# Feature-major stages of a two-block transformer kernel: the wide and the low product change places in every odd step of a tile

## The chip, the cores and the metric

The kernel runs on one core of one Trainium2 chip. The metric is the time of one execution in microseconds on the device. The kernel before took 3048.95 us, the median of three runs (3046.32 to 3049.08).

## The reference, cut to what matters

256 tokens of width 2048 go through two blocks in float32. The first block has a mixer of three kinds of attention, a gated feed-forward with a short convolution (`(gelu(conv(x @ w_gate)) * (x @ w_up)) @ w_down`, inner width 5632) and a gated extra projection. The second has stick-breaking attention and a state-space scan, and then a retrieval of experts (PEER): a query projection `q = (xt @ w_query)` with 2048 columns, scores against keys, a top-16, and the chosen rows of two tables of 16384 x 2048.

Two dense products matter here:

```
hg = x @ w_gate ; x @ w_up      # (256 x 2048) @ (2048 x 5632), twice
q  = (xt @ w_query)             # (256 x 2048) @ (2048 x 2048)
```

## The kernel before, in words

**Precision.** Every float32 operand is split into a high part (rounded to the format that TensorE multiplies) and a low part (the rest). A product is the sum of three: high weights with high activations, high weights with low activations, and low weights with high activations. The fourth, low with low, is left out.

**The stream of weights.** All weights come as units of 128 x 1024 floats (512 KB), in one fixed order over the whole kernel (`UNITS`). SyncE starts one DMA per unit into a slot of `raw` (line 546); ScalarE copies it to `whi` (the high part, line 652), VectorE subtracts to get `wlo` (the low part, line 1294), and TensorE waits in `weights(u)` for the low part, at the head of each unit. A unit's slot is free for the next DMA when TensorE has done its last matmul with it (`s_u`).

**The feature-major stages.** The function `fm_tiles` runs over tiles of 128 output features. A tile takes two units, each with eight of the 16 steps k over the 2048 input features. The result of a tile lies in one bank of PSUM, 128 features by two groups of 256 tokens. `fm_unit` is the function that writes the matmuls of one unit. In each step k it issues two, each with a weight load of its own:

- the wide one: high weights against the high and the low activations side by side, 512 columns, into the whole bank;
- the low one: low weights against the high activations, 256 columns, into the first half of the bank.

VectorE adds the two halves afterwards. Two stages use `fm_unit`: GU, the gate and up projection of the first block, with 88 tiles (line 2451), and WQ, the query projection of the second, with 16 tiles (line 2654). In GU the activations come from the tile `aa`, where the high and the low part lie apart; in WQ from `parts`, where they lie side by side. In both the weights are `whi` and `wlo`.

In steps 0 to 14 of a tile the wide matmul is issued first and the low one second. In step 15 the order is turned, because the last matmul of a tile has to be the one that writes the whole bank. So a tile ends with low 14, low 15, wide 15, and the next starts with wide 0.

The other stages have their own functions and aren't touched: `plain_unit` (all matmuls of 256 columns), `row_unit` (all of 512 columns), and `dn_unit` in the stage D of the second block, which has the same two kinds of product as `fm_unit`, of 384 and 192 columns, in the same order.

TensorE works its instructions off in the order written. Besides the unit it has small jobs of attention, transposes and the like, which `tasks.tick()` puts between units; in GU there are nearly none of them, in WQ there are some after every second tile or so.

Of the kernel before, what the change touches and what calls it, by code (L numbers as in the profile page):

```python
# [231 lines left out]
def build(nc, x, pT, colsd, w1fm, w1v, wo1, wgu, wdn, plg, plp, w2fm, w2v, wo2, wq, sk, dn, dnr, up, g5, out):  # L232
    ctx = ExitStack()
    with ctx:
# [191 lines left out]
        def parts(m, k):  # L426

            return PARTS[k] if m == 4 else AA[:, :, k, :]
# [1716 lines left out]
        def _(e):  # L2145
            tasks = Tasks()

            def mm(o, l, r, start=True, stop=True):
                return e.matmul(o, l, r, start=start, stop=stop)  # L2149
# [9 lines left out]
            def weights(u):  # L2159
                e.wait_ge(s_lo[SLOT[u]], TURN[u])  # L2160
                return WHI[SLOT[u]], WLO[SLOT[u]]
# [66 lines left out]
            def fm_unit(bank, free, m=None):  # L2228


                def unit(u, i, kh):
                    if kh == 0 and free(i) is not None:
                        e.wait_ge(*free(i))
                    w = weights(u)
                    b = B[bank(i)]
                    for kk in range(8):
                        k = kh * 8 + kk
                        hi, lo = [a[:, kk * 128:(kk + 1) * 128] for a in w]
                        if m is not None and i == 0:
                            e.wait_ge(n_al, 16 * m + k + 1)  # L2240
                        p = parts(m, k)
                        if k < 15:
                            mm(b, hi, p, k == 0, False)
                        last = mm(b[:, 0:256], lo, p[:, 0, :], False, False)
                        if k == 15:
                            last = mm(b, hi, p, False, True)
                    last.then_inc(s_u, 1)
                return unit

# [582 lines left out]
```

## Time and profile before

| | |
|---|---|
| median of three runs | 3048.95 us |
| span of the profiled execution | 3047.8 us |
| TensorE matmul busy | 3019.0 us (99%) |
| TensorE weight load busy | 2693.8 us (88%) |
| VectorE busy | 2318.9 us (76%) |
| ScalarE busy | 1676.8 us (55%) |
| mean granted TensorE clock | 0.999 |
| stage GU | from 468.7 to 966.4 us |
| stage WQ | from 1714.5 to 1815.2 us |

How to read it: the span is the time from the first to the last instruction of the one execution that the profiler recorded; for that execution no other time is given, and the runs behind the median are other executions. The weight load is a row of its own, since it runs beside the matmuls. A matmul's recorded duration includes its way through the array, so that consecutive ones overlap: what a matmul costs in a stream is the distance from its start to the start of the next.

### The profile page before, as it was taken

How to read it: one execution, taken by the hardware profiler on the slowest of the kernel's cores; microseconds unless marked ns; L12 is line 12 of the kernel's file. 1: busy time of each engine (PE TensorE's matmuls, PEld its weight loads, DVE VectorE, ACT ScalarE, POOL GpSimd, SP SyncE). 2: the span in 40 equal slices, each digit the busy share in tenths (PEclk: the TensorE clock that was granted, in tenths of full speed). 3: DMA queues.
4: the chain of work that ended last, by engine and by line, in shares of the span. 5: the costliest groups of instructions: out<-in, count | busy, mean ns of one | idle time of the engine just before them, and what ended most of it. 6: DMA issues, size and time to landing. Idle time of an engine off the chain costs nothing.

```text
span 3047.8 us, 44217 instructions
## 1 busy us (share of the span) xinstructions
PE 3019.0 (99%) x17678; PEld 2693.8 (88%) x17678; DVE 2318.9 (76%) x3482; ACT 1676.8 (55%) x2495; POOL 482.3 (16%) x316
## 2 busy tenths in 40 slices
PE   8999999999999999999999999999999999999999
PEld 7999988888888888889898889999999988888887
DVE  5477667777776454567767699999898898999987
ACT  5454655444444344554465545699965555555544
POOL 1000000000000000000000000033222333766642
PEclk9999999999999999999999999999999999999999
DMA  6543445555555555555344656788889999999996
GB/s 220 186 160 124 143 165 178 187 185 187 186 186 190 197 189 187 190 185 178 125 145 159 215 174 226 263 289 292 275 313 353 361 353 358 406 387 384 392 388 257
DMA packets 199213, 726.82 MB, mean 238 GB/s; under 512 B 22240, under 2 KB 22368, under 8 KB 198496
## 3 DMA queue, kind: packets, MB, share of 16 engines
q1 hardware_dynamic: 161280, 585.44, 54.0%
q0 software_dynamic: 37360, 136.79, 12.2%
q8 instruction: 141, 2.31, 0.3%
q10 hardware_dynamic: 368, 1.75, 0.2%
q14 instruction: 64, 0.52, 0.0%
HBM read 719.24 MB, written 4.19 MB: 237 GB/s over the span
## 4 chain that ended last, share of the span: by engine, by line
PE 91%; DVE 5%; ACT 2%; DMA 2%; issue 0%; SPq 0%; DVEq 0%; ACTq 0%
PE b L2149 90%; DVE wlo L1294 2%; DMA raw<-in_dn 1%; PE b L2157 1%; DVE ar L1283 1%; ACT ar L648 1%; ACT whi L652 1%; ACT oh L648 1%; DVE ar L1291 0%; DVE ar L1875 0%; DVE ar L1870 0%; DMA raw<-in_up 0%; DVE ar L1883 0%; DMA hsb<-in_x 0%; DVE ar L1867 0%
## 5 line engine op out<-in xcount | busy, mean ns | idle before, releaser
L1294 DVE TENSOR_TENSOR wlo<-raw,whi 128x1024 fp32r<-128x1024 f32 x1030 | 1251.4, 1222 | 489.1 <-ACT whi L652 485.8
L2149 PE MATMUL b<-aa,whi 128*128 128x256 f32 (+2 forms) x5824 | 1524.4, 340 | 4.3 <-DVE wlo L1294 4.3
L652 ACT ACTIVATE whi<-raw 128x1024 fp32r<-128x1024 f32 x1030 | 1075.8, 1055 | 666.1 <-DMA raw<-in_up 188.8
L2149 PE MATMUL b<-aa,wlo 128*128 128x256 f32 (+1 forms) x4640 | 1211.6, 269 | 0.0
L2149 PEld LDWEIGHTS b<-aa,whi 128*128 128x128 f32 x5824 | 1008.8, 190 | 75.2 <-issue 13.6
L2149 PEld LDWEIGHTS b<-aa,wlo 128*128 128x128 f32 x4640 | 882.0, 190 | 8.7
L2149 PE MATMUL b<-whi,asb 128*128 128x512 f32 x1092 | 366.2, 389 | 1.1 <-DVE ex L1283 1.1
L2149 PE MATMUL b<-whi,aa 128*128 128x512 f32 x1024 | 323.4, 393 | 2.1 <-DVE aa L1294 1.1
L638 POOL DMA_INDIRECT aaf<-in_up,ex x128 | 273.2, 2134 | 158.4 <-DVE aaf L1291 155.0
L2149 PE MATMUL b<-wlo,asb 128*128 128x512 f32 x728 | 283.2, 389 | 0.0
L627 POOL DMA_INDIRECT hsb<-in_dnr,ex x128 | 186.9, 1460 | 463.1 <-DVE small L2057 454.2
L2149 PEld LDWEIGHTS b<-whi,asb 128*128 128x128 f32 x1092 | 204.9, 188 | 44.0 <-DVE ex L1283 1.5
L2149 PEld LDWEIGHTS b<-whi,aa 128*128 128x128 f32 x1024 | 192.2, 188 | 43.1 <-issue 1.7
L648 ACT ACTIVATE ar<-ar 128x512 f32<-128x512 f32 (+5 forms) x212 | 112.3, 539 | 194.1 <-DVE ar L1291 117.2
L603 POOL MEMSET ar<- 128x384 f32 x1 | 0.4, 419 | 1309.5 <-ACT ar L649 1309.5
L2149 PE MATMUL b<-wlo,aa 128*128 128x512 f32 x512 | 199.3, 389 | 0.0
L1291 DVE SCALAR_TENSOR_TENSOR aaf<-aaf,ex 128x1024 f32<-128x1024 f32 x128 | 163.7, 1279 | 0.4 <-DMA aaf<-in_up,ex 0.3
L652 ACT ACTIVATE ar<-b 128x512 f32<-128x512 f32 (+2 forms) x99 | 53.0, 540 | 198.3 <-PE b L2149 163.0
L2149 PEld LDWEIGHTS b<-wlo,asb 128*128 128x128 f32 x728 | 136.7, 188 | 28.3
L2057 DVE CUSTOM_DVE_ANT_0 hsb<-hsb 128x1024 f32<-128x1024 f32 x128 | 155.8, 1218 | 0.1
L2149 PE MATMUL b<-whi,hth 128*128 128x512 f32 x352 | 137.1, 390 | 0.0
L2149 PE MATMUL b<-whi,htl 128*128 128x512 f32 x352 | 137.0, 389 | 0.0
(194 smaller groups left out, 2977.4 us busy)
## 6 DMA issues: line engine op xcount, KB each, us to landing
raw<-in_dn SPq DMA_DIRECT2D x256, 512.0 KB
raw<-in_up SPq DMA_DIRECT2D x182, 512.0 KB
raw<-in_wgu SPq DMA_DIRECT2D x176, 512.0 KB
raw<-in_wdn SPq DMA_DIRECT2D x88, 512.0 KB
raw<-in_w1fm SPq DMA_DIRECT2D x74, 512.0 KB
raw<-in_w2fm SPq DMA_DIRECT2D x74, 512.0 KB
raw<-in_wo SPq DMA_DIRECT2D x64, 512.0 KB
hsb<-in_up SPq DMA_DIRECT2D x44, 512.0 KB
```

What stands on the lines that cost most here:

```text
L603: e.memset(SM, 1.0).then_inc(s_m2, 1)
L627: e.indirect_dma_start(GBD[g % 3], None, dnr, bass.IndirectOffsetOnAxis(ap=IDX[:, g:g + 1], axis=0)).then_inc(s_gd[g % 3], 16)
L638: e.indirect_dma_start(GBU[g % 4], None, upr, bass.IndirectOffsetOnAxis(ap=IDX[:, g:g + 1], axis=0)).then_inc(s_gu[g % 4], 16)
L648: return e.activation(o, i, f, bias=bias, scale=scale)
L652: return e.activation(o, i, ACT.Copy)
L1283: return e.tensor_tensor(o, a, b, op)
L1291: return e.scalar_tensor_tensor(out=o, in0=a, scalar=s, in1=b, op0=op0, op1=op1)
L1294: return e.tensor_tensor(o, a, high.bitcast(F32), ALU.subtract)
L2057: e.tensor_tensor_reduce(GBD[g % 3], GBD[g % 3], HS, 1.0, 0.0, ALU.mult, ALU.add, DOT[:, g:g + 1]).then_inc(s_dot, 1)
L2149: return e.matmul(o, l, r, start=start, stop=stop)
L2157: return e.transpose(o, i, ident[0:n, 0:n])
```

## The change

Within a tile the order of the two matmuls of a step alternates: in even steps the wide one first, in odd steps the low one first. Step 15 is odd and stays as it was. Seven steps of a tile are turned: 1, 3, 5, 7, 9, 11 and 13. The matmul that signals the end of a unit (`last`) is in step 7 now the wide one. Nothing else is changed: neither the number of matmuls and weight loads, nor their operands, nor any wait.

```
@@ -2239,11 +2239,11 @@
                         if m is not None and i == 0:
                             e.wait_ge(n_al, 16 * m + k + 1)
                         p = parts(m, k)
-                        if k < 15:
+                        if k % 2 == 0:
                             mm(b, hi, p, k == 0, False)
                         last = mm(b[:, 0:256], lo, p[:, 0, :], False, False)
-                        if k == 15:
-                            last = mm(b, hi, p, False, True)
+                        if k % 2:
+                            last = mm(b, hi, p, False, k == 15)
                     last.then_inc(s_u, 1)
                 return unit
```

## Rows read from the trace of the kernel before

**Rows 1.** The page: span, and the chain that ended last, by engine.
```profile
span 3047.8 us, 44217 instructions
PE 91%; DVE 5%; ACT 2%; DMA 2%; issue 0%; SPq 0%; DVEq 0%; ACTq 0%
```

**Rows 2.** Windows (PE, PEld, DVE, ACT, POOL busy; clock; DMA): 81 tiles of GU.
```profile
502.86:960.78 457.92, 457.92 (x2593) 397.14 (x2592) 330.71 (x447) 212.31 (x284) 0.00 (x0) 1.00 0.54 186
```

**Rows 3.** The DMA queue's waits from 480 to 960 us (total, times, longest).
```profile
SPq L546 <- PE b L2149: 422.3, 170, 2.9
```

**Rows 4.** Timeline (start us, duration us): twelve steps inside a GU tile.
```profile
503.21 0.40 PE L2149 MATMUL b<-aa,whi 128*128 128x512 f32 x1
503.45 0.28 PE L2149 MATMUL b<-aa,wlo 128*128 128x256 f32 x1
503.56 0.40 PE L2149 MATMUL b<-aa,whi 128*128 128x512 f32 x1
...
507.45 0.40 PE L2149 MATMUL b<-aa,whi 128*128 128x512 f32 x1
```

**Rows 5.** Timeline: the first and the last of 82 tile ends in GU.
```profile
502.15 0.40 PE L2149 MATMUL b<-aa,whi 128*128 128x512 f32 x1
502.39 0.40 PE L2149 MATMUL b<-aa,wlo 128*128 128x256 f32 x2
502.63 0.63 PE L2149 MATMUL b<-aa,whi 128*128 128x512 f32 x2
503.10 0.28 PE L2149 MATMUL b<-aa,wlo 128*128 128x256 f32 x1
...
960.31 0.40 PE L2149 MATMUL b<-aa,wlo 128*128 128x256 f32 x2
960.55 0.63 PE L2149 MATMUL b<-aa,whi 128*128 128x512 f32 x2
961.02 0.28 PE L2149 MATMUL b<-aa,wlo 128*128 128x256 f32 x1
```

**Rows 6.** Timeline: the fourth tile of GU, and the first steps of the fifth.
```profile
486.71 0.39 PE L2149 MATMUL b<-aa,whi 128*128 128x512 f32 x1
486.94 0.28 PE L2149 MATMUL b<-aa,wlo 128*128 128x256 f32 x1
...
490.87 0.39 PE L2149 MATMUL b<-aa,whi 128*128 128x512 f32 x1
491.10 0.40 PE L2149 MATMUL b<-aa,wlo 128*128 128x256 f32 x2
491.33 0.62 PE L2149 MATMUL b<-aa,whi 128*128 128x512 f32 x2
491.79 0.28 PE L2149 MATMUL b<-aa,wlo 128*128 128x256 f32 x1
```

**Rows 7.** Timeline of the weight loads beside the matmuls of Rows 4.
```profile
502.87 0.19 PEld L2149 LDWEIGHTS b<-aa,wlo 128*128 128x128 f32 x1
503.22 0.19 PEld L2149 LDWEIGHTS b<-aa,wlo 128*128 128x128 f32 x1
503.45 0.19 PEld L2149 LDWEIGHTS b<-aa,whi 128*128 128x128 f32 x1
```

**Rows 8.** Timeline: a tile end of stage D, columns 384 and 192.
```profile
1907.29 0.36 PE L2149 MATMUL b<-aa,whi 128*128 128x384 f32 x1
1907.48 0.25 PE L2149 MATMUL b<-aa,wlo 128*128 128x192 f32 x1
1907.57 0.36 PE L2149 MATMUL b<-aa,whi 128*128 128x384 f32 x1
1907.77 0.36 PE L2149 MATMUL b<-aa,wlo 128*128 128x192 f32 x2
1907.96 0.54 PE L2149 MATMUL b<-aa,whi 128*128 128x384 f32 x2
1908.34 0.25 PE L2149 MATMUL b<-aa,wlo 128*128 128x192 f32 x1
```

**Rows 9.** Timeline: twelve wide matmuls in a row in the stage after GU.
```profile
966.67 0.39 PE L2149 MATMUL b<-wlo,hth 128*128 128x512 f32 x1
...
969.39 0.39 PE L2149 MATMUL b<-wlo,hth 128*128 128x512 f32 x1
```

**Rows 10.** Timeline: twelve matmuls of 256 columns in a row.
```profile
1501.92 0.28 PE L2149 MATMUL b<-aa,wlo 128*128 128x256 f32 x1
1502.05 0.40 PE L2149 MATMUL b<-aa,whi 128*128 128x256 f32 x2
...
1503.37 0.28 PE L2149 MATMUL b<-aa,wlo 128*128 128x256 f32 x1
```

**Rows 11.** The chain in order of time, from 1700 to 1850 us (stage WQ).
```profile
1780.17 9.38 PE b L2149 x56
1790.81 1.23 DVE ar L1283
1813.57 1.05 DVE ar L1875 x5
```

More of the change, by code:

```diff
@@ L2241, in unit @@
                         p = parts(m, k)
-                        if k < 15:
+                        if k % 2 == 0:
                             mm(b, hi, p, k == 0, False)
                         last = mm(b[:, 0:256], lo, p[:, 0, :], False, False)
-                        if k == 15:
-                            last = mm(b, hi, p, False, True)
+                        if k % 2:
+                            last = mm(b, hi, p, False, k == 15)
                     last.then_inc(s_u, 1)
```

## The prediction

> **What bounds the kernel now.** I read the page's chain first: TensorE holds 91% of it and waits for little [rows 1]. Then I looked at where the change sits. In a window over 81 tiles of GU, TensorE's matmuls are busy for all of the 457.92 us at a granted clock of 1.00, while VectorE is busy for 330.71 and ScalarE for 212.31 [rows 2]. The DMA queue stands waiting for TensorE for 422.3 of 480 us there [rows 3]: a slot comes free late, not a transfer. So in GU the time is the sum of the distances from one matmul's start to the next one's, and everything else has slack. A nanosecond per step is a nanosecond of the kernel. In WQ the same holds until about 1790 us; from there to 1815 us the chain runs over VectorE, whose work for the search of the top 16 has begun [rows 11]. There about four of the 16 tiles are covered, and a gain or a loss in them counts for less. I keep all 104 tiles in the sums and so overrate either sign by at most 4%.
>
> **What the change does, part by part.** It adds and removes no matmul, load, DMA or wait. Write W for a wide matmul and N for the low (narrow) one. A tile was W N, fifteen times, then N W; it becomes W N N W, eight times. Per tile, with the step over into the next tile:
>
> - before: W to N 15, N to W 15, N to N 1, W to W 1;
> - after: 8 of each kind.
>
> So in each of 88 + 16 = 104 tiles seven W-to-N and seven N-to-W steps go, and seven N-to-N and seven W-to-W steps come: 728 of each. What counts is the price of the four kinds.
>
> *The steps that go.* Inside a tile twelve pairs (wide and low) take from 503.21 to 507.45 us, so 4.24 / 12 = 0.3533 us a pair [rows 4]. A single distance swings by some ns (0.24 and 0.11, then others), in a pattern that repeats after three pairs.
>
> *The steps that come.* The trace of before holds them already, once at each tile end, in the very surroundings that the change makes everywhere: W N N W W N. From the first of the two lows to the first of the two wides (502.39 to 502.63) N-to-N and N-to-W take 0.24 us together; from there over the two wides to the next low (502.63 to 503.10) W-to-W and W-to-N take 0.47 [rows 5]. Over the 82 tile ends from the first to the last shown the means are 240.0 and 469.2 ns, 709.2 together. Two ordinary pairs take 706.7. By this the new order costs 2.5 ns for each group of four matmuls that it adds: 728 x 2.5 ns = +1.8 us.
>
> *The check by whole tiles.* 81 tiles, each with one such tile end, take 457.92 us: 5.653 us a tile, 0.3533 a pair [rows 2]. That is the pace of the twelve pairs that hold no tile end [rows 4]. So whatever the four distances lose is won back in the next ones, and the group costs nothing. The two-decimal starts leave 0.01 us in 4.24 open, 0.8 ns a pair, so 13 ns for the tile end as the difference of 16 pairs. By this the change is 0, with bounds of 728 x 13 ns = 9.5 us on both sides.
>
> I take the middle of the two readings, +1 us (0.03%).
>
> *The loads.* Each load starts with the matmul before its own: the low one's load at 503.22 with the wide at 503.21, the next wide's at 503.45 with the low at 503.45 [rows 4, 7]. So a load is at most one matmul ahead, and behind two low ones in a row each load still has one low matmul to hide under. Is a low matmul long enough? In stage D, with 192 columns, it is not quite: the pair of lows at the tile end takes 0.19 us to the wide (1907.77 to 1907.96), where a single low takes 0.09 (1907.48 to 1907.57), so the second costs about 0.10 to 0.11 [rows 8]. I read about 0.11 us as the least distance that a load allows. In GU a low matmul of 256 columns takes 0.12, in the pair at the tile end (0.24 for two) as in a stream of nothing but such matmuls (1501.92 to 1503.37 for twelve) [rows 5, 10]. The load has about 0.01 us to spare, and stays hidden. Were that cover gone, each N-to-N step would cost what it lacks; D shows the size, 0.02 us over a single one.
>
> *Signals.* In step 7 the last matmul of a unit becomes the wide one. It starts some 0.11 us earlier than the low one did and lasts 0.40 instead of 0.28 [rows 4], so the slot is given back within 0.01 us of before, and the queue behind it has slack [rows 3]. Cost nothing. The waits of the first tile stand ahead of both matmuls of a step, and the banks, which VectorE and ScalarE read, are written last by the same matmul as before.
>
> **Sum.** The profiled execution has a span of 3047.8 us; +1 gives 3048.8. The median of the runs is 1.15 above that span, so I forecast 3050.0 us. Against 3048.95 that is no change: below 0.2%, 6.1 us, a measurement of this kernel hardly tells one from none.
>
> **The rivals.**
>
> *A, the fast lock (faster).* The same alternation also exists at another pace. In the fourth tile of GU twelve pairs take from 486.71 to 490.87 us, 0.3467 a pair, 6.7 ns less; its tile end and what follows, from the first low to the low of the next tile (491.10 to 491.79), take 0.69 against 0.71 [rows 6, 5]. It is the pace at which neither kind loses anything: a stream of wides runs at 2.72 / 12 = 0.2267 us each, a stream of lows at 0.12, together 0.3467 [rows 9, 10]. So the slow pace is a loss of mixing, and the trace went out of the fast pace at a tile end, with the order that the change multiplies. If the new order stays in the fast pace: 104 x 16 x 6.7 ns = 11.1 us less, 3038 us. For it: both paces come with the same instructions, and half of the steps will be of one kind. If only the changes of kind lose, 7 of 15 of this goes, 5 us. Against it: at 82 tile ends in a row the slow pace survived, and the tile end there shows no gain of its own.
>
> *B, steps of one kind at the bare price of the columns (faster).* By the rows the added W-to-W and N-to-N steps take 0.235 and 0.12. The least that they could take is the price of their columns alone; the two streams differ by 0.2267 - 0.12 = 0.1067 us for 256 columns [rows 9, 10], so 0.107 and 0.213: 0.320 a pair instead of 0.353, so 728 x 33 ns = 24 us less, 3025 us. But the streams of one kind themselves don't reach it. The Trainium skill, page "TensorE: Matmul & The Clock Gate", section "Back-to-back issue gap", gives N/2.4 + 2.5 ns for the distance at full clock, so 215.8 and 109.2 ns; by it the change would give 728 x 28 ns = 20 us. The trace doesn't agree: it has 226.7 and 120 in streams of one kind, and it is these that the added steps can hope for.
>
> *C, the bad phase at every group (slower).* The pattern of three pairs has one wide-to-low distance of about 0.24 (502.15 to 502.39, just before the two lows) [rows 5]. After the two wides it is short, about 0.23, which is why the tile end comes out even. The place is the W-to-N step of each group; if it stays at its long value when groups follow each other without the ordinary pairs between, a group costs 0.240 + 0.240 + 0.236 = 0.716 instead of 0.7067. With 8 groups in 104 tiles: 832 x 9.4 ns = 7.8 us more, 3057 us. It decides as soon as a group costs more than 0.714 us (0.7067 + 6.1 / 832). For it: at the tile end four distances, 502.15 to the second wide, do take 0.716, and the recovery is seen only in ordinary pairs behind, of which the new order has none. Against: the pattern is not tied to k, and a lost phase was always won back.
>
> *D, the load exposed (slower).* As in stage D, 0.024 us (0.111, the second low's distance, less 0.087, a single one's; both lie within the two-decimal starts) lost at each second low and nothing regained behind it: 728 x 24 ns = 17 us, 3066 us. In stage D itself the loss is regained at the wides that follow: from 1907.96 over two wides 0.38, where two single ones take 0.40 [rows 8]. And in GU the low is longer than the load. Hardly.
>
> That the change doesn't do what it says can be left out: the order is written out, and TensorE keeps it.
>
> **How the numbers follow.** Forecast (between A and C) 0.58, A 0.20, B 0.02, C 0.15, D 0.03, and 0.02 left for other things. A in its half form falls below 0.2% and counts with no change. Faster by over 0.2%: A and B and a little, 0.23; slower: C, D, 0.18; the rest, 0.59, is no change. Range: 3037 to 3057, which takes in A and just C, the bounds of 9.5 us around the forecast as well; the forecast's own range is 3045 to 3054.
>
> **What would show each step.** In the profile of the changed kernel the timeline of GU must read W, N N, W W, N N, with distances of 0.23 to 0.24 and 0.12. GU must last 497.7 us, give or take 2, and a window of 457.92 us hold 2592 matmuls within ten. The loads must still start with the matmul before their own. If a group of four takes 0.693, A is right; at 0.716, C. If N-to-N is above 0.125, the load shows through. If the time changes while the groups stay at 0.707, the cause lies outside these stages, and my account of them as the only place is wrong.

## The result and the profile after

The changed kernel takes 3039.34 us, the median of 21 runs (3036.18 to 3044.73), against 3047.62 for the kernel before in as many runs. The ratio is 0.9974, with a 95% interval of 0.9969 to 0.9980: 8 us faster, within 6 to 9.5. I had forecast 3050.0 and no change; rival A, the fast lock, had said 3038 and been given one chance in five.

The profiled execution took 3039.05 us, with a span of 3037.3. The chain stands as in [rows 1]: TensorE has 91% of it. Where the time went can be read from the start of each stage. The fences below give these starts. The first is GU's (start, duration). The second has three groups, each with the shortest, middle and longest duration in ns and the first and last start in us: the last stage from 2448.9, the stage after GU from 962.0, WQ from 1710.0. The third is the first product of D, at 1811.48.

```profile
470.97 0.47 PE L2149 MATMUL b<-aa,whi 128*128 128x512 f32 x1
```

```profile
L2149 PE MATMUL b<-whi,asb x1092: 388/389/497, 2448.9 to 3030.0; 128*128 128x512 f32 x182
...
L2149 PE MATMUL b<-whi,hth x352: 389/389/476, 962.0 to 1202.5; 128*128 128x512 f32 x176
...
L2149 PE MATMUL b<-parts,whi x256: 389/396/481, 1710.0 to 1809.6; 128*128 128x512 f32 x128
```

```profile
1811.48 0.41 PE L2149 MATMUL b<-aa,whi 128*128 128x384 f32 x1 [1.44 <-DVE wlo L1294]
```

| stage | before, us | after, us | difference |
|---|---|---|---|
| up to GU (from the first product, at 11.74 and 11.91 us) | 456.9 | 459.1 | +2.1 |
| GU | 497.8 | 491.0 | -6.8 |
| between GU and WQ | 748.1 | 748.1 | 0.0 |
| WQ, to the start of D | 102.15 | 101.44 | -0.7 |
| D | 642.4 | 637.5 | -4.9 |
| the rest (to the start of the last product) | 584.8 | 584.4 | -0.4 |

GU and WQ, the stages of the change, give 7.5 us. The other differences lie in code that is the same in both, and the experiments below show how much they vary by themselves.

Inside GU the window over 80 tiles (columns as in [rows 2]) and the timeline of one of them read:

```profile
504.96:950.83 445.87, 445.87 (x2562) 389.03 (x2560) 326.31 (x440) 209.44 (x280) 0.00 (x0) 1.00 0.55 189
```

```profile
504.73 0.63 PE L2149 MATMUL b<-aa,whi 128*128 128x512 f32 x2
505.19 0.40 PE L2149 MATMUL b<-aa,wlo 128*128 128x256 f32 x2
505.43 0.63 PE L2149 MATMUL b<-aa,whi 128*128 128x512 f32 x2
505.89 0.39 PE L2149 MATMUL b<-aa,wlo 128*128 128x256 f32 x2
506.12 0.62 PE L2149 MATMUL b<-aa,whi 128*128 128x512 f32 x2
```

445.87 / 80 is 5.573 us a tile, where [rows 2] had 5.653: 80 ns less, 88 tiles of them 7.0 us. A group of two lows and two wides takes 0.697 us, the tile divided by eight (504.73 to 506.12 has two groups, 1.39); at the tile ends of before it had taken 0.709 [rows 5]. TensorE is busy for the whole window in both kernels and the granted clock is 1.00, so nothing waits less: the same matmuls follow each other more closely.

### The profile page after: what moved, and what is told of

Its sections match the earlier page's. It is cut to its first block, busy times and chain, and to the rows that moved or that the text cites. A ratio compares the mean times of both kernels' runs of the same rounds, so it can differ in the third digit from the quotient of the medians.

```text
span 3037.3 us, 44217 instructions
## 1 busy us (share of the span) xinstructions
PE 3011.9 (99%) x17678; PEld 2689.8 (89%) x17678; DVE 2320.4 (76%) x3482; ACT 1678.6 (55%) x2495; POOL 468.8 (15%) x316
## 4 chain that ended last, share of the span: by engine, by line
PE 91%; DVE 5%; ACT 2%; DMA 2%; issue 0%; SPq 0%; DVEq 0%; ACTq 0%
PE b L2149 91%; DVE wlo L1294 2%; DMA raw<-in_dn 1%; PE b L2157 1%; ACT whi L652 1%; ACT ar L648 1%; DVE ar L1283 1%; DVE ar L1291 0%; DVE ar L1875 0%; DVE ar L1870 0%; ACT oh L648 0%; DVE ar L1883 0%; DVE ar L1867 0%; DVE ar L1878 0%; DMA hsb<-in_x 0%
## 5 line engine op out<-in xcount | busy, mean ns | idle before, releaser
L2149 PE MATMUL b<-aa,whi 128*128 128x256 f32 (+2 forms) x5824 | 1474.7, 339 | 4.7 <-DVE wlo L1294 4.7
L2149 PE MATMUL b<-aa,wlo 128*128 128x256 f32 (+1 forms) x4640 | 1106.4, 268 | 0.0
L2149 PEld LDWEIGHTS b<-aa,whi 128*128 128x128 f32 x5824 | 963.6, 190 | 18.7 <-issue 13.6
L638 POOL DMA_INDIRECT aaf<-in_up,ex x128 | 262.0, 2047 | 170.8 <-DVE aaf L1291 167.4
```

Of the source, the lines that this page charges most:

```text
L638: e.indirect_dma_start(GBU[g % 4], None, upr, bass.IndirectOffsetOnAxis(ap=IDX[:, g:g + 1], axis=0)).then_inc(s_gu[g % 4], 16)
```

## The experiments

I write W for a wide matmul and n for a low one (N in the recorded expectations). All tile times below are distances between tile starts in the timeline. In GU these repeat from tile to tile within 1 ns once a tile or two of an order have passed, so that one kernel could test eight orders in ranges of eleven tiles; the few orders and widths in which two values alternate are named. The kernels e1 to e7 ran once each, for their profiles, and their whole times are not compared.

Three theories: MIX, a price on each change between wide and low; LOAD, the weight load of a wide is badly covered by a low; LOCK, the matmuls settle into a pattern in time, whose loss depends on order, lengths and phase together and goes by no simple count.

**Eight orders (e1).** `fm_unit` takes its sixteen matmuls of a unit from a list instead of from the loop (excerpt; the function that writes the lists is left out):

```
-                        if k < 15:
-                            mm(b, hi, p, k == 0, False)
-                        last = mm(b[:, 0:256], lo, p[:, 0, :], False, False)
-                        if k == 15:
-                            last = mm(b, hi, p, False, True)
+                        if kind == "W":
+                            last = mm(b, hi, p, k == 0, n == 15 and kh == 1)
+                        else:
+                            last = mm(b[:, 0:256], lo, p[:, 0, :], False, False)
```

> One kernel with eight orders of W (wide) and N (low) in GU, eleven tiles each, every one a permutation of the same matmuls: (0) as before; (1) low first in steps 1 to 15, so one N N and one W W a tile, at another place; (2) step 7 turned beside 15, two groups a tile; (3) steps 3, 7, 11 turned, four groups; (4) as in the changed kernel, eight groups; (5) W W N N for every two steps; (6) W W N N N N W W, runs of four; (7) eight W, sixteen N, eight W. Known: (0) 5.653 us a tile, (4) 5.573; without any loss a tile would be 16 x 0.3467 = 5.547. Theory MIX (each change of kind costs, 0.0067 us for two of them beyond the bare prices): the loss goes with the number of changes, (0) 30, (1) 30, (2) 28, (3) 24, (4) 16, (5) 14, (6) 8, (7) 2 a tile: 5.653, 5.653, 5.646, 5.631, then 5.603 for (4), which the changed kernel already undercuts, 5.575 and 5.553. Theory LOCK (the loss belongs to a pattern of three pairs into which a long alternation falls; a group breaks it): one extra group a tile may already break it, (2) and (3) between 5.55 and 5.60 at once and not in proportion; (1) either 5.653 or 5.547, by the phase; (4) to (7) 5.55 to 5.575 with no further order among them. Theory LOAD (a low gives too little cover to the load of a wide, so N to W costs, N to N not): the loss goes with the number of N-to-W steps, the same list as MIX, but (7) has its W W and N N runs at 0.2267 and 0.120 exactly and the one N-to-W step long.

Measured, eight tiles of each range (the first window has four):

```profile
505.27:527.88 22.61, 22.61 (x130) 19.61 (x128) 16.31 (x22) 10.47 (x14) 0.00 (x0) 1.00 0.57 187
544.83:590.00 45.17, 45.17 (x257) 39.24 (x256) 32.64 (x45) 20.93 (x28) 0.00 (x0) 1.00 0.56 186
606.92:652.04 45.12, 45.12 (x257) 39.23 (x256) 32.63 (x44) 20.93 (x28) 0.00 (x0) 1.00 0.58 186
668.99:714.22 45.23, 45.23 (x258) 39.23 (x256) 32.63 (x45) 20.94 (x28) 0.00 (x0) 1.00 0.57 186
731.02:775.61 44.59, 44.59 (x258) 38.90 (x256) 32.62 (x44) 20.94 (x28) 0.00 (x0) 1.00 0.58 189
792.35:837.10 44.75, 44.75 (x257) 39.09 (x256) 32.63 (x45) 20.94 (x28) 0.00 (x0) 1.00 0.58 188
853.92:898.83 44.91, 44.91 (x258) 39.24 (x257) 32.63 (x44) 20.92 (x28) 0.00 (x0) 1.00 0.59 187
915.59:960.12 44.53, 44.53 (x258) 39.35 (x256) 32.62 (x45) 20.92 (x28) 0.00 (x0) 1.00 0.59 189
```

| order | changes of kind a tile | us a tile | over the lossless 5.5467, in steps of 0.00667 us |
|---|---|---|---|
| (0) as before | 30 | 5.6533 | 16 |
| (1) low first in 1 to 15 | 30 | 5.6467 | 15 |
| (2) one group more | 28 | 5.6400 | 14 |
| (3) three groups more | 24 | 5.6533 | 16 |
| (4) the changed kernel | 16 | 5.5733 | 4 |
| (5) WWnn | 14 | 5.5933 | 7 |
| (6) WWnnnnWW | 8 | 5.6133 | 10 |
| (7) 8 W, 16 n, 8 W | 2 | 5.5667 | 3 |

MIX falls: three groups more gain nothing, seven more gain twelve steps, and eight changes cost more than sixteen. LOAD predicted the same list and falls with it. LOCK had the kind of answer right, but most of its values were wrong: (1) is neither 5.653 nor 5.547, (2) and (3) lie above the 5.55 to 5.60 it gave, since one or three groups more don't break the pattern, and (5) and (6) lie above its 5.55 to 5.575. What I had not asked for: every stable tile time is a whole number of steps of 1/150 us over the lossless 16 x 0.3467 us.

**Eight more orders (e5).** The same edit, other lists.

> Eight more orders of the same matmuls in GU, eleven tiles each (W wide, N low; both units of a tile alike unless said): (0) W NNNNNNNN WWWWWWW, 4 changes of kind a tile; (1) WWWW NNNNNNNN WWWW, 4; (2) WNNNWWWNNNWWWNNW, 12; (3) WWNNNWWWNNNWWNNW, 12; (4) WNWNNWNWWNWNNWNW, 24; (5) WNNWWNWNNWWNWNNW, 20 to 22; (6) the first unit as in the changed kernel, the second as before; (7) the other way round. Theory MIX, already hurt by the orders with 24 and 8 changes that took 5.653 and 5.613 us: (0) and (1) 5.553, (2) and (3) 5.58, (4) 5.63, (5) 5.62, (6) and (7) 5.613, the mean of 5.653 and 5.573. Theory LOCK: every tile time is a whole number of 0.00667 us, between 5.547 and 5.66, with no order by the number of changes; (6) and (7) differ from each other or from 5.613 by at least one such step, and one order at least with 12 or more changes is quicker than one with 4.

| order (each unit) | changes of kind a tile | us a tile | steps |
|---|---|---|---|
| (0) W, 8 n, 7 W | 4 | 5.5867 | 6 |
| (1) 4 W, 8 n, 4 W | 4 | 5.5867 | 6 |
| (2) WnnnWWWnnnWWWnnW | 12 | 5.5733 | 4 |
| (3) WWnnnWWWnnnWWnnW | 12 | 5.5933 | 7 |
| (4) WnWnnWnWWnWnnWnW | 24 | 5.6000 | 8 |
| (5) WnnWWnWnnWWnWnnW | 20 | 5.5933 | 7 |
| (6) changed kernel's, then before's | 22 | 5.6067 | 9 |
| (7) before's, then the changed kernel's | 24 | 5.6200 (5.6167 and 5.6233 by turns) | 11 |

Two windows of this profile, of the ranges (0) (four tiles) and (2) (eight tiles), give 5.5875 and 5.574:

```profile
504.10:526.45 22.35, 22.35 (x130) 19.66 (x128) 16.32 (x22) 10.46 (x14) 0.00 (x0) 1.00 0.54 188
...
604.64:649.23 44.59, 44.59 (x258) 38.90 (x257) 32.61 (x44) 20.94 (x28) 0.00 (x0) 1.00 0.54 190
```

The three marks of LOCK came, two of them with a limit. The tile times are whole steps, but in (7) only the mean of the two alternating values is; each of them lies half a step off. (6) and (7) are two steps apart, but they don't hold quite the same halves: in (6) the half of before ends with its tile end n n W, in (7) it ends with a low, so (7) has two changes of kind more. The third is the clear one: an order with twelve changes is quicker than two with four.

**A kick (e6).** The order of before, and ahead of one tile in eleven a matmul more, whose result the next one discards:

```
+                    if m == 1 and kh == 0 and i % 11 == 5:
+                        c = [32, 64, 96, 128, 160, 192, 224, 256][i // 11]
+                        mm(b[:, 0:c], w[0][:, 0:128], parts(m, 0)[:, 0, 0:c], True, True)
```

> The order of before everywhere, but ahead of the sixth tile of each range of eleven in GU one matmul more, whose result the next one discards, with 32, 64, 96, 128, 160, 192, 224 and 256 columns: a shift of the phase and nothing else. Theory LOCK: the tile with it takes 5.653 plus 0.11 to 0.12 and a remainder that depends on the width without order; after it one tile or more may run at another pace, down to 5.560 as the fourth tile of GU does in the profile of before, and then the tile end leads back to 5.653. Theory MIX or LOAD: 5.653 in every tile but those eight, and in those the plain price of the matmul.

The tiles behind a kick are otherwise those of before. The tile with the kick and the three after it, in us: 32 columns 5.766, 5.654, 5.653, 5.653; 64 columns 5.765, 5.643, 5.561, 5.651; 96 the same but for 1 ns; 128 and 160 columns 5.669, 5.651, 5.653, 5.654; 192 columns 5.682, 5.560, 5.651, 5.654; 224 columns 5.768, 5.561, 5.651, 5.653; 256 columns 5.669, 5.561, 5.650, 5.654. The tile ends around the kick of 64 columns (start, duration; between consecutive ones lies a tile):

```profile
558.89 0.40 PE L2188 MATMUL b<-aa,wlo 128*128 128x256 f32 x2
559.13 0.74 PE L2188 MATMUL b<-aa,whi 128*128 128x512 f32 x3
...
564.66 0.40 PE L2188 MATMUL b<-aa,wlo 128*128 128x256 f32 x2
...
570.29 0.40 PE L2188 MATMUL b<-aa,wlo 128*128 128x256 f32 x2
...
575.86 0.40 PE L2188 MATMUL b<-aa,wlo 128*128 128x256 f32 x2
...
581.51 0.40 PE L2188 MATMUL b<-aa,wlo 128*128 128x256 f32 x2
```

The distances between the starts of the lows are 5.77, 5.63, 5.57 and 5.65: two tiles behind the kick, the very same instructions run in 5.57 us (5.561 from start to start), 0.09 less than their 5.653, and then fall back. This is the experiment that the theories MIX and LOAD can't take in, since neither has a memory. The added matmul lengthens its tile by 0.11 us at 32, 64, 96 and 224 columns, and by 0.016 to 0.03 at 128, 160, 192 and 256. These four are not cheaper matmuls: the rest of their tile runs at the quick pace. With 128 columns twelve pairs behind the kick take 4.16 us, 0.3467 a pair:

```profile
684.56 0.39 PE L2188 MATMUL b<-aa,whi 128*128 128x512 f32 x1
...
688.72 0.39 PE L2188 MATMUL b<-aa,whi 128*128 128x512 f32 x1
```

Less a quick tile of 5.561, these four tiles leave 0.108 to 0.121 us for the kick, and the other four, less a slow one of 5.653, 0.112 to 0.115. So every kick but that of 32 columns changed the pace, in its own tile or behind it. The tile end of before, with its nnWW, is where the pace changes by itself, and it works both ways: at 64, 96 and 224 columns a slow tile ends and a quick one begins, as between the third and the fourth tile of GU in the profile of before (5.643, then 5.560); at 192 and 256 one quick tile follows another; and each of the tiles of 5.560 or 5.561 is followed by one of 5.650 or 5.651, as in [rows 6]. What it does depends on where in the pattern it falls.

**Other widths (e2 in the order of before, e3 in that of the changed kernel).**

```
-                            last = mm(b[:, 0:256], lo, p[:, 0, :], False, False)
+                            wide = [256, 128, 192, 224, 288, 320, 384, 512][i // 11] if m == 1 else 256
+                            r = p[:, 0, :] if m != 1 else aa[:, k * 256:k * 256 + wide]
+                            last = mm(b[:, 0:wide], lo, r, False, False)
```

> The order of before in all tiles; in GU the low matmul streams 256, 128, 192, 224, 288, 320, 384 and 512 columns, eleven tiles each. Below 256 columns the product of low weights with the last tokens is left out; above 256 the columns past 256 add a small wrong product. Bare price of a tile = 16 x (0.2267 + 0.0133 + columns/2400 us), and where the load is the limit at least 0.111 for the low. Theory LOAD: the loss over that price is there at 256 and below and is gone from about 288 on, since a longer low covers the load fully. Theory MIX: the same 0.0067 us a pair at every width from 256 up. Theory LOCK: the loss comes and goes with the width without an order (zero at some widths, up to 0.007 or more a pair at others), because the pattern depends on how the two lengths fit together; at 512, where all are alike, zero in all three.

> As the kernel with the widths 256, 128, 192, 224, 288, 320, 384, 512 of the low matmul, the same parts left out, but with the order of the changed kernel. Theory LOAD: at 128 to 224 columns, where the load is the limit, the order changes nothing; from 288 on neither. Theory MIX: half the loss of the other order at each width from 256 up. Theory LOCK: at some widths the new order gains, at some it loses.

| columns of the low one | bare pair, ns | before's order | changed order |
|---|---|---|---|
| 128 | 337.7 | 341.3 | 343.3 |
| 192 | 337.7 | 342.5 | 340.0 |
| 224 | 337.7 | 343.1 | 343.3 |
| 256 | 346.7 | 353.3 | 348.3 |
| 288 | 360.0 | 364.0 | 364.2 |
| 320 | 373.3 | 379.2 | 376.7 |
| 384 | 400.0 | 413.3 | 413.3 |
| 512 | 453.3 | 453.3 | 453.3 |

(The bare pair is 226.7 for the wide and, for the low, the greater of 111 and columns / 2.4 + 13.3 ns; where tiles alternate between two values, at 192 and 288 in the order of before, their mean stands. At 224 columns in that order the tile is stable at 5.490 us, half a step off the whole steps that the orders of e1 and e5 keep to.) The windows for 384 columns, eight tiles each, e2 and then e3:

```profile
857.96:910.87 52.91, 52.91 (x258) 46.83 (x256) 32.64 (x44) 20.93 (x28) 0.00 (x0) 1.00 0.49 159
```

```profile
857.24:910.15 52.91, 52.91 (x257) 46.72 (x256) 32.63 (x44) 20.93 (x28) 0.00 (x0) 1.00 0.49 159
```

LOAD is out: at 384 columns the low takes at least 173 ns and the load needs 111, which leaves it some 60 ns to spare, and the loss is the greatest of all. MIX is out again. The gain of the new order is there at 192, 256 and 320 columns, not at 224, 288 and 384, and there is a small loss at 128. LOCK's zero loss at some width came true only at 512, where all are alike.

**Shorter loads (e4).**

```
+                        cut = ["", "W", "N", "WN"][i // 11 % 4] if m == 1 and 0 < k < 15 else ""
+                        c = 64 if kind in cut else 128
-                            last = mm(b, hi, p, k == 0, n == 15 and kh == 1)
+                            last = mm(b[0:c, :], hi[:, 0:c], p, k == 0, n == 15 and kh == 1)
-                            last = mm(b[:, 0:256], lo, p[:, 0, :], False, False)
+                            last = mm(b[0:c, 0:256], lo[:, 0:c], p[:, 0, :], False, False)
```

> GU in eight ranges of eleven tiles. Tiles 0 to 43 with the order of before, 44 to 87 with that of the changed kernel; in each, steps 1 to 14 with (0) full loads, (1) the wide's load cut to 64 of its 128 columns, (2) the low's load cut to 64, (3) both. The outputs of the features 64 to 127 lack those products. Theory LOAD: (1), which shortens the load hidden under the low, brings the tile to 5.55 in the order of before, (2) leaves it at 5.653. Theory MIX: no range differs from its full loads, 5.653 and 5.573. Theory LOCK: a change of any load's length can shift the pattern, (1) and (2) alike; in the order of the changed kernel little is left to gain, 5.547 to 5.573.

In the order of before: full loads 5.653 us a tile, the wide's load halved 5.480, the low's halved 5.553, both 5.480. In the changed order: 5.573, 5.507, 5.613, 5.587. The window of the changed order with the low's load halved, eight tiles, is longer than the one with full loads ahead of it:

```profile
723.96:768.55 44.59, 44.59 (x258) 38.90 (x256) 32.62 (x44) 20.93 (x28) 0.00 (x0) 1.00 0.58 189
...
845.92:890.83 44.91, 44.91 (x257) 36.02 (x256) 32.62 (x44) 20.92 (x28) 0.00 (x0) 1.00 0.56 187
```

The weights' shape does take part. LOAD had said 5.55 for the wide's load in the order of before and nothing for the low's; LOCK had left 5.547 to 5.573 for the changed order, and all three cuts fell outside it. Halving the low's load, which has the whole wide to hide under, takes 100 ns off a tile in one order and adds 40 in the other; no account of cover does that. The edit can't part two things: a matmul with half of the load also writes only 64 of the 128 features. I read the difference as the load's, and that is not shown. And the 5.480 lies under what I called lossless: with a half load of a wide to come, a low takes 0.113 us instead of 0.120. So the 0.0133 us that each matmul costs over its columns seems to be partly the next load's. My "lossless" is the best that was seen with full loads in a stream of one kind, and no floor for shorter ones.

**One width (e7).** Steps 1 to 14 with both matmuls of the same width:

```
+                        if m == 1 and 0 < k < 15:
+                            c = [240, 248, 256, 264, 272, 288, 384, 500][i // 11]
+                            last = mm(b[:, 0:c], hi if kind == "W" else lo, aa[:, k * 256:k * 256 + c], False, False)
```

> In GU steps 1 to 14 issue two matmuls of equal width instead of 512 and 256: 240, 248, 256, 264, 272, 288, 384 and 500 columns, eleven tiles each (the outputs are then not the reference's). It measures the distance in a stream of one width. If the distance is columns/2400 + 0.0133 us, it is 0.1133, 0.1167, 0.1200, 0.1233, 0.1267, 0.1333, 0.1733, 0.2217. Theory LOCK with a grid of 0.00667 us on single matmuls: rounded up to 0.1133, 0.1200, 0.1200, 0.1267, 0.1267, 0.1333, 0.1733, 0.2267. Theory MIX and LOAD have no grid.

The mean distances inside a unit (its first and last three left out), in ns: 111.8, 114.1, 119.2, 121.9, 125.8, 131.7, 173.5, 226.7. The first six ranges are shorter than VectorE's work on the weights and come in stretches of a unit, so that the pattern may have no time to settle (the waits for VectorE are 37.4 us between 480 and 880); they are averages over a few matmuls and, if anything, a little under the formula. They don't round up to whole steps, as LOCK with a grid had it: 264 columns were to give 126.7 ns and gave 121.9. Of the two ranges that had time to settle, 384 columns lie on a whole step by the formula too, so that they decide nothing. But 500 columns take the same 226.7 as 512, 5 ns above the formula, which does look like rounding up. I can't say from this what is rounded. About the load: at 240 columns the mean distance is 112 ns, and D's second low took 0.11 [rows 8]. The Trainium skill, page "TensorE: Matmul & The Clock Gate", section "LDWEIGHTS (loading the stationary operand)", gives columns of the weights / 1.2 GHz, by which 128 columns take an estimated 107 ns. The runs show 111 to 112 as the least mean distance of lows in a row, so they agree to about 5 ns; the recorded duration of a load is longer, 0.19 us [rows 7]. Behind a wide a low can be shorter still, 0.09 in D [rows 8].

**The timed ones.** Four kernels on one chip, 11 runs each, against 33 of the kernel before (median 3047.39 us).

e8, the new order in GU alone: `low_first = k == 15 or (m == 1 and k % 2 == 1)`.

> The new order in the 88 tiles of GU alone; WQ as before. All theories that count the gain where the tiles show it (88 x 80 ns): 7.0 us less than before, ratio 0.9977; in the profile GU 491.0 us for 497.8 and WQ 102.1. Rival SPILL (part of the 8.3 us between the medians comes from the later stages, which start in another phase or with other buffers): clearly less or more than 0.9974, or the stage D shorter than 636 us in the profile.

e9, eight wides, sixteen lows, eight wides in GU and WQ, the order (7) of e1:

> Eight wides, sixteen lows, eight wides in each tile of GU and WQ: 5.567 us a tile in the earlier look, 87 ns under before. LOCK and MIX both: 104 x 87 ns = 9.0 us less than before, less what the first tile loses by having to wait for all eight of its high parts first and what VectorE covers in WQ, so 7.5 to 8.5 us, ratio 0.9973 to 0.9976; against the changed kernel no difference that can be measured.

e10, the changed kernel with the same change in `dn_unit`:

```
-                    if k < 15:
+                    if k % 2 == 0:
                         both(False)
                     last = mm(b[:, 0:ND], lo, AH[:, k, TS:256], False, False)
-                    if k == 15:
-                        last = both(True)
+                    if k % 2:
+                        last = both(k == 15)
```

> The changed kernel, and the same order in the 128 tiles of stage D as well, where the low matmul has 192 columns and the weight load is what limits it. The tile of D took 4.554 us, 0.2846 a pair, against 0.1733 + 0.111 = 0.2844 bare: nothing is left to gain by order. LOAD: 4.554 in each order, time as the changed kernel. LOCK: 4.55 to 4.65, so 0 to 12 us more where TensorE sets the pace of D. MIX: no less than 4.550.

e11, the changed kernel as it is:

> The changed kernel again, on the same chip as the three above and timed beside them: ratio 0.9974 to before within 0.0006, by its record of 21 runs; GU 491.0 us, WQ 101.4.

| kernel | median, us | ratio, 95% interval | GU | WQ | D |
|---|---|---|---|---|---|
| e8, GU alone | 3041.69 | 0.9984 (0.9975 to 0.9993) | 491.01 | 102.14 | 637.7 |
| e9, runs of 8 and 16 | 3041.74 | 0.9980 (0.9971 to 0.9989) | 491.83 | 101.44 | 635.9 |
| e10, D too | 3042.54 | 0.9984 (0.9975 to 0.9993) | 491.01 | 101.43 | 641.4 |
| e11, changed kernel | 3040.17 | 0.9979 (0.9970 to 0.9988) | 491.01 | 101.47 | 636.4 |

The intervals overlap and rank nothing among the four. GU in the profile is exact: 491.01 in each kernel that has the changed order there. What was expected of e8, e9 and e11 lies inside their intervals. e9's tiles are 7 ns quicker still, but its first tile has to wait for eight parts at once and takes 7.10 us instead of 5.67; it is no better a kernel. SPILL is not shown: D's length is 635.9 to 639.2 us in the eleven profiles of kernels whose D is that of before, whatever they do in GU and WQ, and only the profile of before has 642.4. e2 and e6, with the order of before in WQ, have 636.1 and 637.0. So the -4.9 in the first table is most likely that one execution's. The same holds for the stage up to GU, which takes 456.9 or 458.5 to 459.3 from profile to profile, also in kernels that are the same up to there.

e10 shows the other sign. Twenty tiles of D in the profile of the changed kernel, and in e10's:

```profile
2321.45:2412.52 91.07, 91.07 (x642) 91.07 (x641) 79.50 (x103) 50.77 (x60) 29.78 (x21) 1.00 0.96 352
```

```profile
2324.07:2415.80 91.73, 91.73 (x641) 91.73 (x641) 81.19 (x104) 50.39 (x60) 29.65 (x21) 1.00 0.96 351
```

4.553 against 4.587 us a tile: the same edit that gave twelve steps in GU costs five in D. LOAD, which said 4.554, is wrong here too; 33 ns on 128 tiles are 4.3 us at most, and D is 5 us longer than in e11.

## Why the prediction was wrong

**What bounds the kernel** was right: TensorE in GU and WQ, nanosecond for nanosecond. GU's 88 tiles times 80 ns are 7.0 us; the stage lost 6.8 (it was to stay at 497.7 within 2, and took 491.0). WQ's 16 tiles would give 1.3 us at that rate and gave 0.7, so more than the four tiles that I had set aside counted for less. The queue and VectorE followed with no wait of their own; the window of after has VectorE busy for as long per tile as before.

**The steps that come** is the step that failed. I took the group's price from the tile ends [rows 5], 0.709 us, in "the very surroundings that the change makes everywhere". The surroundings were the same for six matmuls (W n n W W n), and that isn't enough. The group costs 0.697 when groups follow each other and 0.709 behind a run of plain pairs, and a tile two tiles behind a kick runs 0.09 us faster with nothing changed in it (e6). The steps that stayed moved as well. From the starts in ns, a W-to-N and an N-to-W step together took 353.2 before and 349.2 after, and an N-to-N and a W-to-W step 355.8 before and 347.5 after. Of the 80 ns a tile some 40 lie in the seven pairs of steps that became steps of one kind, 32 in the eight pairs that still change kind, and 8 in the N-to-N and W-to-W step of the tile end, which were there before. The price of a matmul here has a memory over more than a tile; a price read in one stream can't be carried into another.

**The check by whole tiles** was sound arithmetic, and told only that a tile end does not disturb the slow pattern. I read it as "a group costs nothing", with bounds of 9.5 us from the two decimals. The gain of 7.5 was inside these bounds, which is luck.

**The loads** were right in part: each has its matmul to hide under, and no N-to-N step shows the load. Rival D is out. But that the loads matter in no other way was probably wrong (e4, as far as it parts them from the features written).

**Rival A** was right in sign, place and kind: the same instructions have a quick and a slow pace, and the new order leaves the slow one. Its price was 11.1 us for all of the loss; twelve of the sixteen steps went, 80 of 107 ns a tile. Its half form, by the share of changes of kind, is refuted (e1). What weighed against it in my text, 82 slow tile ends in a row, was no evidence about a stream of another make.

**Rival B**: refuted by its price; an N-to-N and a W-to-W step take 114.6 and 232.9 ns in the changed kernel, where it had 107 and 213. But single steps of one kind do get below their stream: the N-to-N steps lie between 113 and 116 ns, where a stream of lows has 120. The W-to-W steps, 232 to 234, lie above the 226.7 of theirs, and the two together, 347.5, don't undercut the two streams' 346.7. **Rival C**: refuted for this stage; no order of sixteen was slower than before's. In D such a loss did appear, 33 ns a tile (e10), so the kind of risk was real.

The forecast of +1 us, with 0.59 for no change, gave too much weight to a local price. Between two known paces, 5.560 and 5.653, for one and the same instruction sequence, the honest answer would have been that either could come, and a kernel with both orders in ranges of tiles would have decided it.

What makes the pattern stays open. The runs show that its loss comes in steps of 1/150 us a tile, 16 cycles at the 2.4 GHz that a granted clock of 1.00 is; that the columns of the matmuls enter, and either the length of the loads or the number of features written; that it depends on what ran before. They don't show which part of TensorE keeps that beat, and no run took the other engines away to see whether they have a part in it; that tiles repeat within 1 ns beside their work speaks against it. The Trainium skill, page "TensorE: Matmul & The Clock Gate", section "Back-to-back issue gap", has a distance for the isolated matmul, columns / 2.4 + 2.5 ns at full clock, that depends on the columns alone; by it a pair would take an estimated 325.0 ns in any order. The traces don't agree: with full loads, pairs took 347 to 353.

## What to carry to other kernels

Where TensorE is the bound and matmuls of two widths alternate, their order alone can be worth 1.4% of a stage's time (GU), and the same edit can cost 0.7% of another's (D): try it per stage, in ranges of tiles of one kernel, and read the distance between tile starts. Don't price a step of such a stream from its rare occurrences in another one. And compute the lossless pace (the streams of one width, added up) first: it tells about how much there is to win with the loads as they are, here 107 ns of 5653.

## What the runs showed of the hardware that I had not expected

- The same 32 matmuls and 32 loads take 5.560 or 5.653 us, depending only on what ran before them, at a granted clock of 1.00 and with nothing waiting (e6).
- Stable tile times in GU lie at whole steps of 6.67 ns over 5.547 us: 3, 4, 6, 7, 8, 9, 10, 14, 15 and 16 of them, in sixteen orders; one order alternates between two values around 11. With other widths there is at least one stable time that lies half a step off (224 columns, 5.490 us).
- A stream of 500-column matmuls is as slow as one of 512, 226.7 ns each.
- Halving the weights of the low matmul, whose load has a whole wide to hide under, made a tile 40 ns slower in one order and 100 ns faster in another.
- An added matmul of 128 columns lengthened its tile by 16 ns, one of 32 columns by 113: the first brought the rest of its tile to the quick pace.
